# Experts in order of their token count, every second one with 64 slots and unsplit fp32 weights on TensorE's column halves

## What is computed

```python
group, in_group = argmax(group_logits), logits of that group's 8 experts
top_val, top_idx = lax.top_k(in_group, 2)            # 2 experts for each of 512 tokens
gate = p_grp * softmax(top_val)
# for every expert e, xs = the rows of its tokens:
a = xs @ w_gate[e]          # (n, 1024) @ (1024, 512)
u = xs @ w_up[e]
y = (silu(a) * u) @ w_down[e]                        # (n, 512) @ (512, 1024)
out[token] += gate * y
```

## Time and profile before

| | us |
|---|---|
| median of 3 runs | 1653.58 (1653.08 to 1655.69) |
| span of the profiled execution | 1651.3 |
| first gate matmul of expert 0 | 1061.7 |
| last down matmul of expert 31 done | 1629.6 |
| from the one to the other, divided by 32 | 17.7 |

### The profile page before, as it was taken

The page is one execution under the profiler, slowest core; times in us unless marked ns, Lnnn a source line. Parts: engine busy times, 40 slices in busy tenths (PEclk is TensorE's granted clock), DMA queues, the critical chain, the costliest instruction groups (busy, mean ns, idle before and its releaser), DMA issues.

```text
span 1651.3 us, 20467 instructions
## 1 busy us (share of the span) xinstructions
PE 1609.1 (97%) x8362; PEld 1325.1 (80%) x8362; DVE 1268.9 (77%) x1455; ACT 924.5 (56%) x1078; POOL 258.2 (16%) x178
## 2 busy tenths in 40 slices
PE   6999999999999999999999999999999999999994
PEld 4668876668988989899888778888888888888883
DVE  6654877887568747475799975699999999999994
ACT  6433235543444435352533244688888878888884
POOL 0000021000047232310000100111221221221201
PEclk9999999999999999999999999999999999999997
DMA  8306822004222313231222101599999999999993
GB/s 342 128 1 253 301 94 77 0 0 155 76 102 77 137 68 128 77 128 52 103 77 78 44 34 64 210 419 386 371 371 383 382 357 369 372 373 364 385 366 119
DMA packets 55316, 322.92 MB, mean 196 GB/s; under 512 B 12736, under 2 KB 13760, under 8 KB 18610
## 3 DMA queue, kind: packets, MB, share of 16 engines
q1 hardware_dynamic: 43584, 307.91, 49.0%
q0 software_dynamic: 9504, 8.43, 2.3%
q10 hardware_dynamic: 2130, 5.22, 0.8%
HBM read 323.60 MB, written 23.07 MB: 210 GB/s over the span
## 4 chain that ended last, share of the span: by engine, by line
PE 93%; DVE 2%; DMA 2%; ACT 2%; issue 1%; POOL 0%; SPq 0%; ACTq 0%; DVEq 0%; POOLq 0%
PE ps L586 25%; PE ps L1488 21%; PE ps L1515 11%; PE ps L1101 7%; PE ps L776 5%; PE ps L1357 3%; PE ps L1024 2%; PE ps L752 2%; PE ps L1472 2%; PE ps L809 1%; DMA xT<-in_x 1%; PE ps L1497 1%; PE ps L888 1%; PE ps L1012 1%; ACT whi L1567 1%
## 5 line engine op out<-in xcount | busy, mean ns | idle before, releaser
L2244 DVE TENSOR_TENSOR wlo<-raw,whi 128x2048 fp32r<-128x2048 f32 (+1 forms) x256 | 583.4, 2300 | 123.5 <-ACT whi L1567 123.4
L1567 ACT ACTIVATE whi<-raw 128x2048 fp32r<-128x2048 f32 (+1 forms) x256 | 485.4, 1912 | 146.3 <-PE ps L1488 36.6
L1488 PE MATMUL ps<-whi,xH 128*128 128x512 f32 x512 | 202.7, 396 | 1.3 <-DVE xL L2353 1.3
L1488 PE MATMUL ps<-whi,xL 128*128 128x512 f32 x512 | 200.2, 391 | 0.0
L1488 PE MATMUL ps<-wlo,xH 128*128 128x512 f32 x512 | 199.3, 389 | 0.0
L586 PE MATMUL ps<-hH,whi 128*128 128x512 f32 x352 | 138.7, 394 | 0.3 <-ACT dmax L2050 0.3
L586 PE MATMUL ps<-hH,wlo 128*128 128x512 f32 x352 | 137.1, 390 | 0.0
L586 PE MATMUL ps<-hL,whi 128*128 128x512 f32 x352 | 137.0, 389 | 0.0
L3307 POOL DMA_INDIRECT sum_scratch<-yb,idt x30 | 48.8, 1625 | 422.5 <-ACT yb L2185 408.7
L1488 PEld LDWEIGHTS ps<-whi,xL 128*128 128x128 f32 x512 | 96.1, 188 | 20.8
L1488 PEld LDWEIGHTS ps<-whi,xH 128*128 128x128 f32 x512 | 96.1, 188 | 20.4 <-DVE xL L2353 1.5
(11 more groups left out here) (527 smaller groups left out, 3533.7 us busy)
## 6 DMA issues: line engine op xcount, KB each, us to landing
raw<-in_experts SPq DMA_DIRECT2D x192, 1024.0 KB, 7.7
raw<-in_streamed SPq DMA_DIRECT2D x92, 1024.0 KB, 4.8
xT<-in_x SPq DMA_DIRECT2D x1, 2048.0 KB, 17.1
sum_scratch<-xN ACTq DMA_DIRECT2D x2, 1024.0 KB, 9.1
Y<-sum_scratch SPq DMA_DIRECT2D x4, 512.0 KB, 5.0
out<-Y SPq DMA_DIRECT2D x4, 512.0 KB, 2.7
h_scratch<-hN SPq DMA_DIRECT2D x4, 384.0 KB, 2.6
ctxT<-in_ctx SPq DMA_DIRECT2D x1, 1024.0 KB, 18.4
```

What stands on the lines that cost most here:

```text
L1488: ins = e.matmul(b.t[:, :], l, w, start=(kk == 0 and i == 0), stop=(kk == 7 and i == 2))
L1567: e.activation(u.hi, u.raw, ACT.Copy).then_inc(*p.inc("hi", n, on="hi"))
L2244: e.tensor_tensor(u.lo, u.raw, u.hi.bitcast(F32), ALU.subtract).then_inc(*p.inc("lo", n, on="lo"))
```

## The change

- **Ranking.** In the route part the experts' token counts are turned into ranks (VectorE, with `keyc`, `keyr`), and a permutation matrix `pick` places them: places 0 and 1 stay experts 0 and 1, then the even places take the fullest experts in turn and the odd ones the emptiest. The 16 emptiest have at most 64 tokens each.
- **Tables by place.** Two more groups of 8 matmuls (`by_expert`) make the tables by expert, and 5 small ones (`by_place`), behind the up matmuls of expert 0, permute them to `eid` (which expert stands at a place), `idp`, `gsp` and, for small experts, `idq`, `gsq`. From place 2 on gathers, scatters and gates use them.
- **Loads.** From place 2 on SyncE reads the expert's number from `eid` into a register ahead of each load, and the load's address hangs on it.
- **Small experts** (odd places from 3): 64 slots. Their weights aren't split: the raw load is the matmul's operand and is free when TensorE has used it. Rows are turned to 64 columns (`xS`); gate goes to partitions 0 to 63 and up to 64 to 127 of one PSUM bank, each 8 fp32 matmuls of 512 columns at column offset 0 or 64 of TensorE's array (`pair`). ScalarE copies the bank (`paired`), 4 transposes turn both, sigmoid and the two products work on 256 columns, and down is again 8 matmuls, the left 512 output columns on one half and the right on the other (`down_small`). One scatter of 128 half rows brings them to `sum_scratch`.
- **Order.** Loads of a small expert come as g, u, g, u ahead of d of the one before. Conversions run ahead by three split loads (`use_split`); the unsplit ones don't count.
- The last two experts no longer scatter in halves.

The core of the diff:

```diff
+    def small(x):
+        return x > 2 and x % 2 == 1
+    def pair_units(x):
+        made_ = [expert_unit(what, x, h) for h in range(2) for what in "gu"]
+        return made_[0::2], made_[1::2]
...
+        if small(x):
+            U_E["g", x], U_E["u", x] = pair_units(x)
+        else:
+            U_E["g", x] = expert_units("g", x)
...
-        for what in "du" if x + 1 < NEXP else "ud":
-            U_E[what, x - (what == "d")] = expert_units(what, x - (what == "d"))
+        U_E["d", x - 1] = expert_units("d", x - 1)
+        if not small(x):
+            U_E["u", x] = expert_units("u", x)
...
+        def by_expert():
...
+            for c in range(8):
+                e.matmul(b.t[0:32, 0:128], Ot[:, c, :], R1[:, c, :], start=(c == 0), stop=(c == 7))
+            for c in range(8):
+                ins = e.matmul(b.t[0:64, 128:256], Og[:, c, :], R1[:, c, :], start=(c == 0), stop=(c == 7))
...
+        def pair(x, h):
...
+            p.wait_ge(*done("dve", "xL", x, 0))
+            p.wait_ge(*done("dma", "u", g.n))
+            p.wait_ge(*done("dma", "u", u.n))
...
+                e.matmul(b.t[0:64, :], xS[:, kk, :], g.raw[:, k, :], start=(kk == 0), stop=(kk == 7), tile_position=(0, 0))
+                ins = e.matmul(b.t[64:128, :], xS[:, kk, :], u.raw[:, k, :], start=(kk == 0), stop=(kk == 7),
+                               tile_position=(0, 64))
...
+        def down_small(x):
...
+                    e.matmul(b.t[0:64, :], aS[:, kk, :], u.raw[:, k, 0:512], start=(kk == 0), stop=(kk == 3),
+                             tile_position=(0, 0))
+                    ins = e.matmul(b.t[64:128, :], aS[:, kk, :], u.raw[:, k, 512:1024], start=(kk == 0), stop=(kk == 3),
+                                   tile_position=(0, 64))
...
+        def use_split(n):
+            while split_at[at_[0] - 1] < min(split_at[n] + 3, len(split_order) - 1):
                 convert(at_[0])
...
+        def turn_small(x):
+            p.wait_ge(*done("pe", "x4", x, 0))
+            p.wait_ge(*done("pe", "use", U_E["u", x - 2][1]))
+            copy(xS, ps["x4", x, 0].t[:, :].rearrange("p (d c) -> p d c", d=8), p.inc("xL", x, 0))
...
+        def permute():
+            p.wait_ge(*done("pe", "eid"))
+            TS(eid[:, :], ps["eid",].t[0:1, 0:32], -1.0, None, ALU.add, key=("eid",))
+            p.wait_ge(*done("pe", "place"))
...
+            if x > 1:
+                p.wait_ge(*done("dve", "perm"))
+            n = 64 if small(x) else 128
+            rows = (idt if x < 2 else idp)[0:n, x:x + 1]
...
+            if u.expert:
+                x, i = u.expert
+                p.wait_ge(*done("dve", "eid"))
+                if book.real:
+                    v = e.value_load(eid[0:1, x:x + 1], min_val=0, max_val=NEXP - 1)
+                    view = A["experts"][bass.ds(v, 1), i].rearrange("a p n -> p (a n)")
+            e.dma_start(u.flat, view).then_inc(*p.land("raw%d" % u.place, "u", n))
```

More of the change, by code:

```diff
@@ L431, in build, with expert_unit @@
     MODS = MOD_FIRST
+    def small(x):
+        return x > 2 and x % 2 == 1
+    def expert_unit(what, x, h):
+        k, n = (2, 1024) if what == "d" else (4, 512)
+        i = 2 * "gud".index(what) + h
+        u = stream(A["experts"][x, i] if x < 2 else None, k, n, not small(x))
+        units[u].expert = None if x < 2 else (x, i)
+        return u
     def expert_units(what, x):
-        k, n = (2, 1024) if what == "d" else (4, 512)
-        return [stream(A["experts"][x, 2 * "gud".index(what) + h], k, n) for h in range(2)]
+        return [expert_unit(what, x, h) for h in range(2)]
+    def pair_units(x):
+        made_ = [expert_unit(what, x, h) for h in range(2) for what in "gu"]
+        return made_[0::2], made_[1::2]
     half_ring.insert(0, Place(third.off))
@@ L1440, in pe_program @@
         for j in range(4):
-            ins = e.matmul(b.t[:, 128:160], oneB, AS[:, j, :], start=(j == 0), stop=(j == 3))
+            e.matmul(b.t[:, 128:160], oneB, AS[:, j, :], start=(j == 0), stop=(j == 3))
+        for j in range(4):
+            ins = e.matmul(b.t[0:32, 160:161], AS[:, j, :], oneB[:, 0:1], start=(j == 0), stop=(j == 3))
         ins.then_inc(*p.inc("pos"))
@@ new lines, in by_place @@
+        def by_place():
+            b = ps.take(("eid",), ("dve", "eid"))
+            p.wait_ge(*done("dve", "pick"))
+            p.wait_ge(*done(*b.before))
+            e.matmul(b.t[0:1, 0:32], valt[0:32, 0:1], pick[0:32, :], start=True, stop=True).then_inc(*p.inc("eid"))
+            b = ps.take(("place",), ("dve", "perm"))
+            p.wait_ge(*done("dve", "gT"))
+            p.wait_ge(*done(*b.before))
+            for i, v in enumerate((tT[0:32, 0:128], tT[0:32, 128:256], gT[0:32, 0:128], gT[0:32, 128:256])):
+                ins = e.matmul(b.t[:, 32 * i:32 * i + 32], v, pick[0:32, :], start=True, stop=True)
+            ins.then_inc(*p.inc("place"))
@@ L1523, in pe_program @@
         table(1, 64, Og)
+        by_expert()
         turn_x(1)
         for x in range(NEXP):
-            half_mm(x, "u", 0)
-            half_mm(x, "u", 1)
-            if x + 1 < NEXP:
-                half_mm(x + 1, "g", 0)
-                turn_a(x)
-                half_mm(x + 1, "g", 1)
+            if not small(x):
+                half_mm(x, "u", 0)
+                half_mm(x, "u", 1)
+            if x == 0:
+                by_place()
+            if x + 1 < NEXP:
+                for h in range(2):
+                    if small(x + 1):
+                        pair(x + 1, h)
+                    else:
+                        half_mm(x + 1, "g", h)
+                    if h == 0:
+                        turn_a(x)
             if x == NEXP - 2:
-                half_mm(x + 1, "u", 0)
-                half_mm(x + 1, "u", 1)
                 down(x, lambda: turn_a(x + 1))
@@ L3297, in pool_program @@
             gather(x)
-        for x in range(NEXP - 2):
+        for x in range(NEXP):
             if x + 4 < NEXP:
@@ L3393, in brought_back @@
         p.wait_ge(*done("pe", "use", U_E["d", NEXP - 1][1]))
-        p.wait_ge(*done("dma", "yb", NEXP - 3))
-        for x in range(NEXP - 2, NEXP):
-            for q in range(2):
-                p.wait_ge(*done("dma", "yb", x, q))
+        for x in range(NEXP - 3, NEXP):
+            p.wait_ge(*done("dma", "yb", x))
         for i in range(4):
```

242 lines of the change are left out of this document (177 added, 65 removed).

## The result

The changed kernel takes 1773.39 us (median of three, 1771.77 to 1774.48) against 1653.58: ratio 1.0718, 95% interval 1.0699 to 1.0737. The forecast was 1663.6 with a range of 1630 to 1703. The sign is right, the size is not: 120 us instead of 10, and above the 1740 of rival D, the highest of all, which had a chance of 0.04.

What follows compares the result with a forecast made beforehand. The prediction took TensorE as the bound before, and a loop from one small expert's pair matmuls to the next's after. 13.7 + 12 - 14.7 - 1 = +10.0; 1651.3 + 10.0 + 2.3 = 1663.6 us, range 1630 to 1703.

Steps and rivals of the forecast that it cites:

- rival D: Pair matmuls: fp32 at a column offset takes four passes, halves in turn; 4 pairs 6.9 us, 1740 us; chance 0.04.
- the predicted station: On VectorE: the copy xS of small expert 19 stands behind the subtraction of load 210, holding up its pair matmuls.
- The length of the turn: One turn of the loop, per pair of experts: 36.40 us against 35.42 before; over 14 turns +13.7 us.
- The prediction's own loop: From one small expert's pair matmuls through freed buffer, ten loads, conversion, subtraction and xS to the next's pairs: 36.40 us.
- register load: On SyncE ahead of the loop's first DMA: 0.7 us, the middle between bounds of 0.3 and 1.3.
- four pairs: Pair matmuls on TensorE at the end of a turn: 4 at 0.429, 1.72 us, both column halves at once.
- 12 in 5.15 us, 0.429 each: Price of a full-width fp32 matmul of 512 columns, read from a trace row and used for each pair.
- 213 to 222 landed (ten loads): Loads within a turn: first 4.8 us from issue to landing, nine more at 2.50, token rows 1.8.
- B: Rival: the loop is shorter and the gain shows, 1633 us, or 1605 if only the DMA binds; chance 0.24.
- C: Rival: the two column halves run one after the other, 4 pairs cost 3.43 us; 1690 us; chance 0.24.
- The start, +12: From expert 2 on, gathers and loads wait for the permuted table; load stream 12 us late, TensorE 9 us late.
- The end, -14.7 - 1: TensorE ends 3.7 us after the last landing instead of 18.4, -14.7 us; one scatter instead of two, -1 us.

Runs made afterwards that it cites:

- e9_xs: The changed kernel with VectorE's copy xS of a small expert one split load earlier, ahead of the first down load's subtraction of the expert before: 1751.5 us.
- e5_order2: The changed kernel with the order on VectorE and ScalarE written out for each pair of experts, small operations no longer behind conversions of later loads: 1635.9 us.
- e8_onehalf: The changed kernel without the gate matmuls of small experts but the first, up staying on the other column half: 1770.5 us.
- e1_order: The changed kernel with xS and the small expert's products one split load earlier on VectorE, and sigmoids and scalings moved ahead of conversions on ScalarE: 1746.7 us.
- e2_warm: The changed kernel with filler matmuls, results overwritten: 30 ahead of each pair's first half while TensorE waits, 8 ahead of each down_small: 1752.3 us.

## Why the prediction was wrong, point by point

**The bound before, and that a loop takes its place.** Right. TensorE has gaps (74 to 80 us busy of 100), and what ended last was a chain of waits over conversions running three split loads ahead. e9_xs shows the predicted station at work.

**The length of the turn.** Wrong, 36.4 against 44.5 us in the turn shown. The prediction's own loop, read from the trace: SyncE issues the first load at 1389.71, the tenth from there is converted from 1422.12 on, the pairs run from 1427.01 to 1433.39, and the next first load goes out at 1434.16.

```profile
1389.71 1.43 SPq L3567 DMA_DIRECT2D raw<-in_experts  x2
...
1396.08 4.48 SPq L3567 DMA_DIRECT2D raw<-in_experts  x4
...
1412.90 4.30 SPq L3567 DMA_DIRECT2D raw<-in_experts  x4
```

| step | predicted | measured |
|---|---|---|
| register load | 0.7 | 0.8 |
| ten loads, issue of the first to conversion of the tenth | 4.8 + 22.5 + 1.8 = 29.1 | 32.4 |
| conversion, subtraction, xS | 4.9 | 4.9 |
| four pairs | 1.7 | 6.4 |

Two steps failed.

1. *"12 in 5.15 us, 0.429 each".* Six matmuls, 0.858 each. Four pairs cost 3.4 us at full clock, twice the 1.72 of the sum, and 6.4 at the half clock, to which the new gaps bring them. For the clock the sum had no term at all. Rival D had nearly this figure (6.9), but by way of halves in turn; that it comes close is luck. The Trainium skill's rule on fp32, named above, stood beside the row and contradicted it; I let the row decide without asking what one record is. The 240 of L1536 could not be known, but the loop behind L1024 could be counted.
2. *"213 to 222 landed (ten loads)" as one stream.* It isn't one. The first eight go out by 1400.23 (the last of the x4 from 1396.08 on), the ninth only at 1412.90. The ninth and the tenth take the buffers of the small expert's down loads, which down_small must use first, and down_small waits for aS, which stands behind a subtraction as xS does. This second station puts a landing, a conversion, four pairs and two more register loads on the way; the ten loads take 3.3 us more than in the sum, of which 0.7 are the first one (5.5 us from issue to landing, not 4.8). The prediction looked at what stands behind the subtraction of load 210, and at no other row.

How the 8 us divide between these can't be read off by taking one away at a time. The single edits give 2.7 (price), 2.0 (clock), 1.8 (register) and 1.6 or 2.3 us (order), but they shift the wait to the next station, and price and clock overlap. Only the whole order (e5_order2) opens the loop.

**The rivals.** B was put as "if the order doesn't bind at all and only the DMA's 32.2 does": 1605 with 32.2 us per pair. e5_order2, with the order opened, comes near to it: 33.9 us per pair, and 1636. Of the change as it stands B was wrong. C's premise, halves in turn, is refuted by e8_onehalf; its arithmetic (3.43 for four pairs) is by luck the right one at full clock.

**The start, +12.** The wait for the rows gathered by the table was read rightly: the transposes of expert 2 start at 1091.07, where the sum had 1090.5. The first scatter is 11.6 late, the size of the term, but that is in part luck: some 7 come from the table, and 4.5 remain without it, for which the sum had 2.1 (the matmuls of by_expert) and else nothing. By place 2 it is 20.6, since the order's waits begin there; e5_order2 has 16.6 at place 2 and 13.1 at place 4.

```profile
1091.07 1.97 PE L1575 MATMUL ps<-cst,xg 128*128 128x128 f32 x8 [5.74 <-DMA xg<-h_scratch,idp]
```

**The end, -14.7 - 1.** Nearly right in sum: from the last load's issue to TensorE's last start (1750.30, plus 0.6) it takes 13.1 us, against 26.3 before, -13.2. Two errors offset each other there, which is luck. The load lands in 5.1 us instead of 7.9, and after the landing TensorE needs 8.0 us, not 3.7: the last four pairs cost 3.5 instead of 1.7, and until 1747.33 TensorE is still at the down matmuls of expert 30. The scatters at the end gave nothing: 21.8 us from TensorE's end on, 21.7 before.

**Range and chances.** The range ended at 1703 because its upper edge, C with slower loads, was priced with 0.429 and had neither the clock nor the way by down_small in it. The chance of "slower", 0.62, was on the right side, but with D, the only rival above 1703, at 0.04.

## What to carry to other kernels

Look-ahead counted in a subset of the items (only the split loads) lets the engine that converts run far ahead in the real stream, and everything small that is queued behind a conversion then waits for a load that nobody needs yet. When such a distance changes, list for every small operation which load now stands ahead of it, and follow each loop through the ring of buffers to its end; opening one alone only showed the next here (e9_xs, e1_order). Before a row's count is turned into a price, check it against the loop that issues it.

## What the runs showed of the hardware

- An unsplit fp32 matmul of 512 columns has two records in the trace and takes 0.86 us at full clock, at full width (six in 5.15 us) as well as on 64 columns of weights (four in 3.59); two on different column halves start 6 to 7 ns apart, and four such pairs take 3.58 us, no more than four alone.
- TensorE stood idle for 7.42 us, and the granted clock was 0.50 in the 6 us in which it took up work again and 0.95 in the 6 us behind them. With e2_warm's filler it was 0.98 to 1.00 over stretches of 100 us.
- A register load on SyncE costs 0.72 us of issue distance (1.10 us with it, 0.38 without; in longer bursts of issues 1.11 and 0.37 to 0.48). In e5_order2, where transfers were always queued, moving it ahead of the wait changed nothing (1635.2 against 1635.9 us); in the changed kernel the turn was 1.84 us shorter without it.
- With loads always queued, the DMA engines moved 384 to 394 GB/s, token rows included, at a share of 0.98 to 1.00 (e5_order2), more than the 369 to 378 of the kernel before at 0.99 to 1.00: a share near 1 did not say that no more could be moved.
